# Turning the residual unscaled and by column halves, and scaling the gate and up rows behind the matmul

## The chip, the cores and the metric

One of the eight cores of a Trainium2 chip runs the kernel: TensorE (matmul), VectorE, ScalarE, GpSimd and SyncE, on-chip memory SBUF, and PSUM, eight banks of 128 x 512 floats that TensorE writes. The metric is the device time of one execution in microseconds.

## The reference

Two transformer blocks over 256 tokens of width 1024, all in float32. The first block (three mixers, a mixture of experts and an embedding gate) is not touched. The second has two layers, and each ends in the feed-forward stage that the change is about:

```python
def rmsnorm(x, g):
    var = jnp.mean(xf * xf, axis=-1, keepdims=True)
    return (xf * lax.rsqrt(var + RMS_EPS)).astype(x.dtype) * g

def conv_ffn(h, w_up, w_conv, w_down):
    gu = causal_dwconv(h @ w_up, w_conv)      # 3 taps along the tokens
    g, u = jnp.split(gu, 2, axis=-1)          # D_FF = 2816 columns each
    return (jax.nn.silu(g) * u) @ w_down

for i in range(2):
    h = rmsnorm(x, mix_norm[i])
    x = x + (short_conv_mixer(h, ...) if i == 0 else moba_attention(h, ...))
    x = x + conv_ffn(rmsnorm(x, ffn_norm[i]), ffn_w_up[i], ffn_w_conv[i], ffn_w_down[i])
return rmsnorm(x, final_norm)
```

## The kernel before

Weights come as a stream of 216 units of 128 x 2048 floats. SyncE loads them into four buffers (`raw`). Each matmul is done as three passes of a narrower float format, so each unit is split: ScalarE writes the rounded part `whi`, VectorE the difference `wlo` (`split`, L505 and L1099), into rings of three. A ring slot is free again when TensorE has counted up `unit_used`; a `raw` buffer is loaded again when VectorE has counted up `low_done`. Every engine runs its own list of instructions strictly in order and waits on counters; `split_to(n)` issues all splits up to unit n at that place of the list. The order of all lists is written by hand.

**The turn.** `xres` holds the residual, tokens on partitions, as two tiles of 128 tokens; `add` (L1136) adds a PSUM bank to one half of the columns (512) of one tile. For the next product the residual has to stand with its columns on partitions. So ScalarE squares each half tile and sums it (`norm_act`, L531), GpSimd makes the inverse root `rstd` (`norm_pool`, L1005), VectorE writes `xn = xres * rstd` (`normed`, L1120), TensorE transposes the sixteen 128 x 128 blocks (`turn`, L1869), and ScalarE and VectorE take them out of PSUM with the norm's gain as a high and a low part (`turn_act` L540, `turn_dve` L1126), eight blocks each. Turn 5 stands ahead of feed-forward stage 0 and turn 7 ahead of stage 1.

**The product ahead of a turn.** `dense` (L1896; in the attention layer `o_part`, L2496) makes two chunks of 512 columns, each of two units. Of the second chunk's second unit all products of tile 0 come first (`tile_done`), then those of tile 1 (`unit_used`), so `add_chunks` (L1146) can add the tiles apart.

**A feed-forward stage** (`experts`, L2399) has eleven groups. `group` (L2346) makes 256 gate and 256 up rows from two units: 96 matmuls into two PSUM banks, bank pair by the group's parity. ScalarE then starts the three-tap convolution out of PSUM (L789) and VectorE adds two taps (L1642), 4 + 8 instructions. Then ScalarE's silu, VectorE's product, ScalarE's rounding and VectorE's low part, and `h_ready` lets `down` (L2367) multiply the hidden block by one unit. TensorE's order is group 0, group 1, down 0, group 2, down 1, and so on; `expert_step` (L2391) makes one group and the down product of the group before. ScalarE and VectorE have the unit splits between: `ahead(3)` before a group's convolution, `ahead(4)` behind it, `ahead(5)` behind silu and product. In the first step `ahead(4)` is the second unit of group 1. The last group (`halves_apart`, `ffn_last_act` L802, `ffn_last_dve` L1661) puts the gate and up rows of half 0 in one bank and those of half 1 in the other, and its halves are worked off apart. Ahead of that both engines split unit 32 of the stage, which needs the slot of the last group's first unit.

## Time and profile before

| | |
|---|---|
| median of 3 runs | 1138.96 us (1138.21 to 1139.0) |
| profiled execution | 1140.76 us, its span 1138.9 us |
| TensorE busy | 94% of the span |
| VectorE, ScalarE, GpSimd busy | 74%, 63%, 7% |
| chain that ended last | TensorE 78%, VectorE 13%, ScalarE 4% |
| mean granted TensorE clock | 0.980 of full |

The profiled execution has instruction starts and lengths for every engine. Times count from the span's start. Engines are PE (TensorE), PEld (its weight loads), DVE (VectorE), ACT (ScalarE), POOL (GpSimd), SP (SyncE). A row of the timeline may merge like instructions (x8), and ends, where the engine stood idle before it, with that time and what ended it. A matmul's recorded length includes its way through the array, so matmuls overlap. Stage 0 lies at about 613 to 800 us, stage 1 at 943 to 1131.

### The profile page before, as it was taken

How to read it: one execution, taken by the hardware profiler on the slowest of the kernel's cores; microseconds unless marked ns; L12 is line 12 of the kernel's file. 1: busy time of each engine (PE TensorE's matmuls, PEld its weight loads, DVE VectorE, ACT ScalarE, POOL GpSimd, SP SyncE). 2: the span in 40 equal slices, each digit the busy share in tenths (PEclk: the TensorE clock that was granted, in tenths of full speed). 3: DMA queues.
4: the chain of work that ended last, by engine and by line, in shares of the span. 5: the costliest groups of instructions: out<-in, count | busy, mean ns of one | idle time of the engine just before them, and what ended most of it. 6: DMA issues, size and time to landing. Idle time of an engine off the chain costs nothing.

```text
span 1138.9 us, 17179 instructions
## 1 busy us (share of the span) xinstructions
PE 1076.1 (94%) x6358; PEld 932.5 (82%) x6358; DVE 842.6 (74%) x1084; ACT 713.6 (63%) x947; POOL 76.3 (7%) x82
## 2 busy tenths in 40 slices
PE   7998979999999999889999999999899989999997
PEld 6877867777877787769988899998788868999996
DVE  5498678999899998767654776676867866766765
ACT  6667478888888887665433654454557765554553
POOL 1001100000000000030000110120000011101100
PEclk9999989999999999999999999999999998999999
DMA  9440528888889898645443545554343324555531
GB/s 369 163 161 25 212 82 306 332 333 316 343 320 343 312 352 305 243 157 185 170 168 143 186 173 197 188 185 179 148 148 111 111 96 151 203 198 189 185 142 38
DMA packets 33604, 232.62 MB, mean 204 GB/s; under 512 B 3856, under 2 KB 3984, under 8 KB 6032
## 3 DMA queue, kind: packets, MB, share of 16 engines
q1 hardware_dynamic: 32688, 229.98, 54.6%
q10 hardware_dynamic: 864, 1.93, 0.5%
q8 instruction: 34, 0.56, 0.2%
q14 instruction: 18, 0.15, 0.0%
HBM read 230.85 MB, written 1.05 MB: 204 GB/s over the span
## 4 chain that ended last, share of the span: by engine, by line
PE 78%; DVE 13%; ACT 4%; issue 3%; DMA 2%; POOL 1%; DVEq 0%; ACTq 0%; SPq 0%; POOLq 0%
PE bank L1862 11%; PE bank L1863 11%; PE bank L1864 11%; PE bank L2361 9%; PE bank L2362 9%; PE bank L2363 9%; DVE wlo L1104 5%; PE bank L2218 4%; PE bank L2219 4%; PE bank L2201 2%; DMA raw<-stream 1%; PE bank L2226 1%; PE bank L2267 1%; PE bank L2266 1%; DVE arena L1502 1%
## 5 line engine op out<-in xcount | busy, mean ns | idle before, releaser
L1104 DVE TENSOR_TENSOR wlo<-raw,whi 128x2048 fp32r<-128x2048 f32 x212 | 481.8, 2286 | 85.9 <-ACT whi L514 84.8
L514 ACT ACTIVATE whi<-raw 128x2048 fp32r<-128x2048 f32 x213 | 406.6, 1917 | 122.2 <-PE bank L2363 64.1
L2361 PE MATMUL bank<-xs,whi 128*128 128x256 f32 x896 | 252.2, 282 | 4.5 <-DVE wlo L1104 3.3
L2362 PE MATMUL bank<-xs,whi 128*128 128x256 f32 x896 | 251.3, 280 | 0.0
L2363 PE MATMUL bank<-xs,wlo 128*128 128x256 f32 x896 | 250.8, 280 | 0.0
L2361 PEld LDWEIGHTS bank<-xs,whi 128*128 128x128 f32 x896 | 169.5, 189 | 6.7 <-DVE wlo L1104 3.7
L2362 PEld LDWEIGHTS bank<-xs,whi 128*128 128x128 f32 x896 | 169.6, 189 | 0.8
L2363 PEld LDWEIGHTS bank<-xs,wlo 128*128 128x128 f32 x896 | 169.5, 189 | 0.0
L1862 PE MATMUL bank<-whi,rounded 128*128 128x512 f32 x344 | 139.3, 405 | 5.4 <-DVE rounded L1511 4.9
L1863 PE MATMUL bank<-wlo,rounded 128*128 128x512 f32 x344 | 137.7, 400 | 0.0
L1864 PE MATMUL bank<-whi,rounded 128*128 128x512 f32 x344 | 137.5, 400 | 0.0
L1862 PE MATMUL bank<-whi,xs 128*128 128x512 f32 (+1 forms) x304 | 122.9, 404 | 6.2 <-DVE xs L1625 2.1
L1864 PE MATMUL bank<-whi,xs 128*128 128x512 f32 (+1 forms) x304 | 120.2, 395 | 0.0
L1863 PE MATMUL bank<-wlo,xs 128*128 128x512 f32 (+1 forms) x304 | 120.0, 395 | 0.0
L1646 DVE SCALAR_TENSOR_TENSOR arena<-bank,cwn,arena 128x255 f32<-128x255 f32 (+1 forms) x160 | 66.1, 476 | 68.0 <-ACT arena L790 67.3
L1862 PEld LDWEIGHTS bank<-whi,rounded 128*128 128x128 f32 x344 | 65.7, 191 | 24.5 <-issue 7.5
L790 ACT ACTIVATE arena<-bank,cwn 128x256 f32<-128x256 f32 x80 | 31.4, 476 | 84.8 <-PE bank L2363 84.8
L1864 PEld LDWEIGHTS bank<-whi,rounded 128*128 128x128 f32 x344 | 65.6, 191 | 15.9
L1863 PEld LDWEIGHTS bank<-wlo,rounded 128*128 128x128 f32 x344 | 65.4, 190 | 13.0
L1862 PEld LDWEIGHTS bank<-whi,xs 128*128 128x128 f32 x304 | 58.5, 193 | 19.2 <-issue 3.3
L1864 PEld LDWEIGHTS bank<-whi,xs 128*128 128x128 f32 x304 | 58.2, 192 | 13.4
L1863 PEld LDWEIGHTS bank<-wlo,xs 128*128 128x128 f32 x304 | 58.6, 193 | 11.9
(320 smaller groups left out, 1462.5 us busy)
## 6 DMA issues: line engine op xcount, KB each, us to landing
raw<-stream SPq DMA_DIRECT2D x215, 1024.0 KB, 4.8
arena<-finals ACTq DMA_DIRECT2D x3, 512.0 KB, 3.8
xres<-x_in SPq DMA_DIRECT2D x2, 512.0 KB, 5.0
raw<-stream SPq DMA_DIRECT2D x4, 256.0 KB, 6.2
out<-xn SPq DMA_DIRECT2D x4, 256.0 KB, 2.1
par<-params SPq DMA_DIRECT2D x1, 844.0 KB, 12.5
cst<-table SPq DMA_DIRECT2D x1, 502.0 KB, 8.9
arena<-p_in ACTq DMA_DIRECT2D x1, 256.0 KB, 6.0
```

Of the source, the lines that this page charges most:

```text
L514: act.activation(whi[:, s, :], raw[:, a, :], ACT.Copy).then_inc(S("high_done"), 1)
L790: ins = act.activation(facc[:, b, f, :], bank[2 * gb + f // 2][:, (f % 2) * T:(f % 2 + 1) * T], ACT.Copy, scale=cwn[:, b, 8 + f:9 + f])
L1104: dve.tensor_tensor(wlo[:, s, :], raw[:, unit0 % RAW, :], whi[:, s, :].bitcast(F32), ALU.subtract)\
L1646: ins = dve.scalar_tensor_tensor(a, src[:, 0:T - 2 + k], cwn[:, b, 4 * k + f:4 * k + f + 1], a, ALU.mult, ALU.add)
L1862: pe.matmul(o, ah, bh, start=start, stop=False, skip_group_check=True)
L1863: pe.matmul(o, ah, bl, start=False, stop=False, skip_group_check=True)
L1864: return pe.matmul(o, al, bh, start=False, stop=stop, skip_group_check=True)
L2218: pe.matmul(bank[e][:], tokens, whi[:, s, c], start=kk == 0, stop=False, skip_group_check=True)
L2219: ins = pe.matmul(bank[e][:], tokens, wlo[:, s, c], start=False, stop=kk == 7, skip_group_check=True)
L2361: pe.matmul(o, whi[:, s, w], xhi[:, kk, :], start=first, stop=False, skip_group_check=True)
L2362: pe.matmul(o, whi[:, s, w], xlo[:, kk, :], start=False, stop=False, skip_group_check=True)
L2363: ins = pe.matmul(o, wlo[:, s, w], xhi[:, kk, :], start=False, stop=kk == 7, skip_group_check=True)
```

## The change

- Turns 5 and 7 transpose `xres` itself, not `xn`. They go by column halves: the eight transposes of half 0 stand inside the product ahead (between the units of its second chunk, or between its two tiles), tile 0's other four behind it, tile 1's other four inside group 0, ahead of its block k = 2. `normed` falls away for them.
- The inverse root is put in later. After group 0 TensorE spreads `rstd` along a row of 256 tokens by two matmuls against the identity, and ScalarE copies it out (`root_row`). For every group VectorE multiplies both PSUM banks by this row into `fraw` (two instructions, `rooted`), and all taps read `fraw` in SBUF. TensorE waits for `rooted` instead of `g_free` before it writes the banks again.
- The last group runs in two passes over its two units: first all rows of half 0 (`half_done`), then those of half 1. Its units are let go in the second pass only.
- The splits, adds and turns on ScalarE and VectorE are put in a new order around both turns (below), and two units more are split before the turn or inside it.
- The projection of layer 0 swaps its banks (first chunk 0 and 1, second 2 and 3). Some counters get other names, and the adds of the first block are written out in the order that they had.

```diff
-CHUNK_BANK = {C_PLEG: 0, C_PLEG + 1: 4, C_QKV: 4, C_QKV + 1: 6}
+CHUNK_BANK = {C_PLEG: 0, C_PLEG + 1: 4, C_SCOUT: 0, C_SCOUT + 1: 2, C_QKV: 4, C_QKV + 1: 6}
...
+        fraw = arena[:, 2048:4096].rearrange("p (b f t) -> p b f t", b=2, f=4)
+        root_row = arena[:, 4096:4096 + T]
@@ ScalarE, ffn_act @@
-                act.wait_ge(S("unit_used"), group_end(u0, e, e0))
+                act.wait_ge(S("rooted"), d0 + 1 + e)
...
-                    ins = act.activation(facc[:, b, f, :], bank[2 * gb + f // 2][:, (f % 2) * T:(f % 2 + 1) * T],
-                                         ACT.Copy, scale=cwn[:, b, 8 + f:9 + f])
+                    ins = act.activation(facc[:, b, f, :], fraw[:, b, f, :], ACT.Copy, scale=cwn[:, b, 8 + f:9 + f])
@@ ScalarE, ahead of stage 0 @@
-            split_to(U_SCOUT + 4)
+            split_to(U_FFN0)
+            turn_act(5, range(0, 4))
             norm_act(5, slice(0, 2))
-            split_to(U_SCOUT + 5)
-            norm_act(5, slice(2, 4))
+            split_to(U_FFN0 + 1)
...
+                split_to(u0 + 2)
+                act.wait_ge(S("root_made"), layer + 1)
+                act.activation(root_row, bank[4][:, 0:T], ACT.Copy).then_inc(S("root_ready"), 1)
                 ffn_act(layer, 0, None, 0)
...
-            turn_act(5)
+            turn_act(5, range(4, KD))
+            norm_act(5, slice(2, 4))
             ffn(0)
@@ ScalarE, ahead of stage 1 @@
+            split_to(U_FFN1)
             o_high(7)
-            split_to(U_WO + 4)
-            norm_act(7)
-            split_to(U_WO + 5)
+            split_to(U_FFN1 + 1)
+            turn_act(7, range(0, 4))
+            norm_act(7, slice(0, 2))
+            turn_act(7, range(4, KD))
+            norm_act(7, slice(2, 4))
             act.dma_start(final_g, finals[1]).then_inc(S("final_loaded"), 16)
-            turn_act(7)
             ffn(1)
@@ VectorE, ahead of stage 0 @@
-            add_chunks(U_SCOUT, C_SCOUT, 5, late=True)
+            split_to(U_SCOUT + 3)
+            add_first(C_SCOUT, CHUNK_END[C_SCOUT])
+            split_to(U_FFN0)
+            turn_dve(5, range(0, 4))
+            add_second(C_SCOUT, 5, 0)
+            split_to(U_FFN0 + 1)
+            add_second(C_SCOUT, 5, 1)
+            turn_dve(5, range(4, KD))
@@ VectorE, ffn_dve @@
                 ahead(3)
+                dve.wait_ge(S("unit_used"), group_end(u0, e, e0))
+                if e0 == 0:
+                    dve.wait_ge(S("root_ready"), layer + 1)
+                for half in range(2):
+                    ins = dve.tensor_tensor(fraw[:, b, 2 * half:2 * half + 2, :],
+                                            bank[2 * gb + half][:].rearrange("p (f t) -> p f t", f=2),
+                                            root_row.unsqueeze(1).broadcast_to([P, 2, T]), ALU.mult)
+                ins.then_inc(S("rooted"), 1)
+                dve.wait_ge(S("rooted"), d0 + 1 + e)
                 dve.wait_ge(S("ffn_begun"), layer * FH + 1 + e)
@@ VectorE, ffn_last_dve @@
                 split_to(u0 + 3 * FE - 1)
                 for half in range(2):
+                    dve.wait_ge(*((S("unit_used"), group_end(u0, e, e)) if half else (S("half_done"), layer + 1)))
+                    dve.tensor_tensor(fraw[:, b, half::2, :], bank[2 * gb + half][:].rearrange("p (f t) -> p f t", f=2),
+                                      root_row.unsqueeze(1).broadcast_to([P, 2, T]), ALU.mult)\
+                       .then_inc(S("rooted"), 1)
+                    dve.wait_ge(S("rooted"), d0 + 1 + e + half)
                     dve.wait_ge(S("ffn_begun"), layer * FH + 1 + e + half)
@@ VectorE, ahead of stage 1 @@
+            split_to(U_FFN1)
             o_low(7)
-            add_chunks(U_WO, C_WO, 7, U_WO + 3, late=2)
-            turn_dve(7)
+            add_first(C_WO, U_WO + 3)
+            add_second(C_WO, 7, 0)
+            turn_dve(7, range(0, 4))
+            add_second(C_WO, 7, 1)
             split_to(U_FFN1 + 1)
+            turn_dve(7, range(4, KD))
@@ TensorE @@
+            def turn_tile(q, t, ks):
+
+                for k in ks:
+                    if k % 4 == 0:
+                        pe.wait_ge(S(f"residual{t}_ready"), 2 * q - 1 + k // 4)
+                    ins = pe.transpose(turned_k(q, k)[:, P * t:P * t + P], xres[:, t, P * k:P * k + P], ident)
+                    if t == 1 and k % 2:
+                        ins.then_inc(S("turned"), 1)
@@ group @@
-                for i in range(2):
+                for part_, i in [(p, i) for p in range(2 if halves_apart else 1) for i in range(2)]:
                     s = wait_unit((unit0 + i, off))
                     for k in range(4):
                         kk = 4 * i + k
+                        if kk in ahead_of:
+                            ahead_of[kk]()
                         wait_turned(q, kk)
-                        for at in range(4):
+                        for at in range(2 * part_, 2 * part_ + 2) if halves_apart else range(4):
...
-                    ins.then_inc(S("unit_used"), 1)
+                    if part_ or not halves_apart:
+                        ins.then_inc(S("unit_used"), 1)
+                    elif i:
+                        ins.then_inc(S("half_done"), 1)
@@ expert_step @@
-                pe.wait_ge(S("g_free"), g0 + e)
+                if e0:
+                    pe.wait_ge(S("rooted"), d0 + e)
@@ experts @@
-                group(g0, u0, q)
+                turn_tile(q, 0, range(4, KD))
+                group(g0, u0, q, ahead_of={2: lambda: turn_tile(q, 1, range(4, KD))})
+
+                pe.wait_ge(S("xt_ready"), KD * q + 2)
+                for t in range(TT):
+                    pe.wait_ge(S(f"rstd{t}_ready"), q + 1)
+                    ins = pe.matmul(bank[4][:, P * t:P * t + P], rstd[:, t:t + 1].broadcast_to([P, P]), ident,
+                                    start=True, stop=True, skip_group_check=True)
+                ins.then_inc(S("root_made"), 1)
...
-            for c in range(2):
-                dense(C_SCOUT + c, U_SCOUT + 2 * c, "sc_ready" if c == 0 else None, c == 1)
-            turn(5)
+            dense(C_SCOUT, U_SCOUT, "sc_ready")
+            dense(C_SCOUT + 1, U_SCOUT + 2, None, True, lambda: [turn_tile(5, t, range(4)) for t in range(TT)])
...
             o_part(1, 1, (2, 3), (0,))
+            for t in range(TT):
+                turn_tile(7, t, range(4))
             o_part(1, 1, (2, 3), (1,))
-            turn(7)
```

## Rows read from the trace of the kernel before

**Rows 1.** The page, busy time of each engine over the span.
```profile
PE 1076.1 (94%) x6358; PEld 932.5 (82%) x6358; DVE 842.6 (74%) x1084; ACT 713.6 (63%) x947; POOL 76.3 (7%) x82
```

**Rows 2.** The waits of PE: line, waited-for line, us in total, times, longest.
```profile
PE bank L1884 <- DVE xn L1123: 8.4, 5, 3.9
...
PE bank L2361 <- DVE wlo L1104: 3.3, 2, 1.6
```

**Rows 3.** Timeline of PE at turn 5: start, length, instruction, idle before.
```profile
609.66 1.09 PE L1884 MATMUL bank<-cst,xn 128*128 128x128 f32 x8 [1.18 <-DVE xn L1123]
611.61 1.65 PE L1884 MATMUL bank<-cst,xn 128*128 128x128 f32 x8 [0.85 <-DVE xn L1123]
613.59 0.55 PE L2361 MATMUL bank<-xs,whi 128*128 128x256 f32 x1 [0.32 <-DVE xs L1132]
```

**Rows 4.** Timeline of ACT and DVE around turn 5.
```profile
602.98 1.92 ACT L514 ACTIVATE whi<-raw 128x2048 fp32r<-128x2048 f32 x1 [2.46 <-PE bank L1864]
605.72 0.69 DVE L1138 TENSOR_TENSOR xres<-bank,xres 128x512 f32<-128x512 f32 x1 [4.10 <-PE bank L1864]
...
612.08 3.03 ACT L545 ACTIVATE xs<-bank,par 128x256 fp32r<-128x256 f32 x8 [2.11 <-PE bank L1884]
```

**Rows 5.** Timeline of DVE, PE and ACT at turn 7 and the end of group 0 behind it.
```profile
932.42 2.09 DVE L1138 TENSOR_TENSOR xres<-bank,xres 128x512 f32<-128x512 f32 x3 [2.59 <-PE bank L1864]
...
939.11 3.59 PE L1884 MATMUL bank<-cst,xn 128*128 128x128 f32 x16 [3.92 <-DVE xn L1123]
...
956.04 1.57 ACT L790 ACTIVATE arena<-bank,cwn 128x256 f32<-128x256 f32 x4 [9.75 <-PE bank L2363]
```

**Rows 6.** Timeline of ACT, DVE and PE behind group 0 of stage 0.
```profile
625.89 1.57 ACT L790 ACTIVATE arena<-bank,cwn 128x256 f32<-128x256 f32 x4 [8.97 <-PE bank L2363]
...
627.50 3.34 DVE L1646 SCALAR_TENSOR_TENSOR arena<-bank,cwn,arena 128x255 f32<-128x255 f32 x8 [6.92 <-ACT arena L790]
630.76 2.28 DVE L1104 TENSOR_TENSOR wlo<-raw,whi 128x2048 fp32r<-128x2048 f32 x1
...
633.09 0.38 PE L2361 MATMUL bank<-xs,whi 128*128 128x256 f32 x1 [1.64 <-DVE wlo L1104]
```

**Rows 7.** A PE wait; windows: busy PE, PEld, DVE, ACT, POOL, granted clock, DMA share, GB/s.
```profile
584.30 0.47 PE L1862 MATMUL bank<-whi,xs 128*128 128x512 f32 x1 [2.07 <-DVE xs L1625]
...
585.00:586.00 1.00, 1.00 (x4) 0.81 (x3) 0.95 (x2) 1.00 (x1) 0.00 (x0) 0.50 0.12 49
633.00:634.00 1.00, 0.91 (x7) 0.91 (x8) 1.00 (x3) 0.63 (x2) 0.09 (x1) 1.00 0.00 0
```

**Rows 8.** Timeline of DVE, ACT and PE around the last group of stage 1.
```profile
1108.41 2.28 DVE L1104 TENSOR_TENSOR wlo<-raw,whi 128x2048 fp32r<-128x2048 f32 x1
...
1114.82 1.92 ACT L514 ACTIVATE whi<-raw 128x2048 fp32r<-128x2048 f32 x1 [2.77 <-PE bank L2363]
...
1116.77 2.29 DVE L1104 TENSOR_TENSOR wlo<-raw,whi 128x2048 fp32r<-128x2048 f32 x1 [2.67 <-ACT whi L514]
1121.23 3.47 DVE L1673 SCALAR_TENSOR_TENSOR arena<-bank,cwn,arena 128x255 f32<-128x255 f32 x8 [2.17 <-ACT arena L813]
...
1120.35 1.57 ACT L813 ACTIVATE arena<-bank,cwn 128x256 f32<-128x256 f32 x4 [3.62 <-PE bank L2363]
...
1126.16 0.47 PE L1862 MATMUL bank<-whi,rounded 128*128 128x512 f32 x1 [0.25 <-DVE rounded L1685]
```

**Rows 9.** The page and the groups of lines (count, busy us, mean ns), then one timeline row.
```profile
L1646 DVE SCALAR_TENSOR_TENSOR arena<-bank,cwn,arena 128x255 f32<-128x255 f32 (+1 forms) x160 | 66.1, 476 | 68.0 <-ACT arena L790 67.3
L790 ACT ACTIVATE arena<-bank,cwn 128x256 f32<-128x256 f32 x80 | 31.4, 476 | 84.8 <-PE bank L2363 84.8
...
L867 ACT ACTIVATE arena<-arena,par 128x256 f32<-128x256 f32 x8 | 3.6, 503 | 3.3 <-DVE arena L1606 3.3
L1614 DVE SCALAR_TENSOR_TENSOR arena<-arena,par 128x256 f32<-128x256 f32 x16 | 7.0, 482 | 4.3 <-ACT arena L867 4.2
...
82.88 0.39 PE L2021 MATMUL bank<-arena,cst 128*128 128x128 f32 x2
```

More of the change, by code:

```diff
@@ L538, in norm_act, with turn_act @@
                                    accum_out=sumsq[:, t, c:c + 1]).then_inc(S(f"sumsq{t}_ready"), 1)
-            def turn_act(q):
-                for k in range(KD):
+            def turn_act(q, ks=range(KD)):
+                for k in ks:
                     if k % 2 == 0:
@@ L1124, in normed, with turn_dve @@
                        .then_inc(S(f"xn{t}_ready"), 1)
-            def turn_dve(q):
-                for k in range(KD):
+            def turn_dve(q, ks=range(KD)):
+                for k in ks:
                     if k % 2 == 0:
@@ L1396, in _ @@
             turn_y_dve(2)
-            add_chunks(U_WOUT, C_WOUT, 1, U_WOUT + 3, late=True)
+            split_to(U_WOUT + 4)
+            add_first(C_WOUT, U_WOUT + 3)
+            dve.wait_ge(S("final_loaded"), 16)
+            for t in range(TT):
+                tokens_scaled(t, 0)
+            for t in range(TT):
+                add_second(C_WOUT, 1, t)
+                tokens_scaled(t, 1)
             turn_dve(2)
@@ L1922, in dense @@
                     ins.then_inc(S("unit_used"), 1)
+                    if u == 0 and between:
+                        between()
             pe.wait_ge(S("ident_loaded"), 16)
@@ L2555, in _ @@
             o_part(1, 1, (2, 3), (0,))
+            for t in range(TT):
+                turn_tile(7, t, range(4))
             o_part(1, 1, (2, 3), (1,))
-            turn(7)
             experts(G_FFN1, FH, U_FFN1, FE, 7)
```

86 lines of the change are left out of this document (34 added, 52 removed).

## The prediction

> **What bounds the kernel now.** I read the page's busy shares first. TensorE is busy for 1076 of 1139 us, VectorE for 74% [rows 1]. So relieving VectorE or ScalarE alone can't pay. What can pay is time in which TensorE stands still. The waits of TensorE, read next, show where that is. It waits for `xn` at the transposes five times, 8.4 us in total, and for `wlo` inside the group products twice, 3.3 us [rows 2]. The timeline of the stretches that the diff touches gives the rest.
>
> **Before feed-forward stage 0** the last product of the projection ends at 608.48 (609.66 less 1.18 idle). The first eight transposes start at 609.66, the other eight at 611.61, and the first gate/up product at 613.59 [rows 3]. The two tiles of the projection's second column half end one after the other. Its first half ends at about 602.7, tile 0 at 605.7, and the adds follow [rows 4]. The rest of the pause is squares on ScalarE, the inverse root on GpSimd, and the scaling by it on VectorE. **Before stage 1** it is the same pause, longer: products end at 935.19 (939.11 less 3.92), sixteen transposes run from 939.11 to 942.70, and the group ends at 956.04 [rows 5].
>
> **Inside a stage** the steady step is bound by TensorE: two units of a group and one of a down product, 5.6 us each (the two units of the last group are let go at 1114.82 and 1120.35, the down products end at 1125.91) [rows 6, 8]. A step is 16.8 us. The exceptions are the first step and the last. In the first, the second unit of group 1 can't be split before the taps of group 0, since VectorE has that split behind them: group 0 is handed over at 625.89, the split starts at 630.76, and TensorE goes on at 633.09 after 1.64 us idle [rows 6]. In the last, TensorE waits only 0.25 us for the hidden block [rows 8].
>
> **The change, part by part.** All sums are against the profiled execution, 1140.76 us with a span of 1138.9; the median of the runs shown, 1138.96, lies 1.8 below it, and I carry the difference over to it.
>
> *1. The turn by halves.* Eight transposes take 1.09, the last of them 0.27 long, so one each 0.117 us and eight 0.94 [rows 3]. Eight now stand in the middle of the projection's second half, where their input (column half 0) has been added long before. Four stand behind it and four inside group 0, ahead of its third block of rows. I followed each input. In stage 0 tile 0's second half is ready at 607.4 and needed at 609.4. Tile 1's is late, because VectorE has the split of the group's second unit before that add, and ScalarE's half of that split stands behind four turned blocks (from 603.7, 0.38 each [rows 4]) and two squares (twice as wide, 0.65 each by my estimate). It runs at about 606.5 to 608.4, so VectorE splits until 610.7 and adds until 611.4. TensorE asks at 612.5, so 1.1 us of cover are left; without it each us late costs a us. In stage 1 VectorE adds at once and the cover is 1.6 us. So group 0 should follow the transposes with no pause and at full clock. A group at full clock is 2 x 5.55 us and 0.2 for its last product to leave, 11.3. Its end comes at 608.48 + 0.94 + 0.94 + 11.3 = 621.7 instead of 625.89, and at 935.19 + 1.88 + 11.3 = 948.4 instead of 956.04 [rows 5, 6]. **Gain 4.2 + 7.7 = 11.9 us.** The clock that is lost now behind these pauses is in it.
>
> *2. Scaling behind the matmul* is not free. For the first group of a stage TensorE spreads the root over the partitions by two fp32 products. One with 128 columns is recorded as two parts, 0.22 together [rows 9], so 0.44. ScalarE copies the row out (0.48, as its other 256-wide evictions [rows 9]). VectorE multiplies two banks; three 128x512 adds out of PSUM take 2.09 [rows 5], so two about 1.35. Only then come ScalarE's four taps and VectorE's eight. All of it is on the chain that sets the split of group 1's second unit: 0.44 + 0.48 + 1.35 + 0.15 for three hand-overs, 2.4 us more. The unit starts 9.6 us after the group instead of 7.2, and TensorE, which has 5.85 us of work, stands for 3.75 us instead of 1.64. The ends of the 2.4 are 1.9, with the spreading products at one pass each like a transpose and the multiplications at 0.48, and 2.8, with 0.1 us lost at each hand-over. I take 2.4, since each term is nearest to its row. **Cost 2.4 x 2 = 4.8 us.** The root itself is squared and raised while group 0 runs (ScalarE and GpSimd have little else there), so it isn't late.
>
> In the steady steps VectorE had three splits, taps and two products, 3 x 2.28 + 3.34 + 2 x 0.69 = 11.6 us of 16.8 [rows 6]; now 12.9. The second unit's split is done 8.8 us after the group and needed at 11.2, the hidden block at 12.3 and needed at 16.8. No cost; the cover is 2.4 us.
>
> The eight taps now read SBUF. The nearest rows are the short convolution's: 482 ns for a tap from SBUF against 476 from PSUM, and on ScalarE 503 against 476 [rows 9]. I take no gain and 0.1 us of loss within the hand-overs. The Trainium skill (VectorE: DVE Perf Modes, "The TRN2 errata") gives VectorE 62 cycles at 0.96 GHz less for an SBUF source than for a PSUM one, and ScalarE 52 cycles at 1.2 GHz more. By that estimate the four tap chains would be 0.35 us shorter each, and the sum 1.4 us lower. The rows agree for ScalarE in direction (+27 ns) and not for VectorE.
>
> *3. The last group in two passes.* Its first pass (gate and up rows of half 0) ends after 5.6 us, which looks like an early start. But both passes need both units. The second unit is wanted 2.8 us into the group instead of 5.6. Its split ended at 1110.69 [rows 8] and is now 1.4 us later, 1112.15, against a need at 1111.75: 0.4 us of stall. And the first unit is let go only at three quarters of the group: 1118.0 instead of 1114.82. Both ScalarE and VectorE have the split of the last down unit (unit 32 of the stage) ahead of everything of the last group. ScalarE's part then ends at 1119.95, VectorE's at 1122.25 (1119.05 now, before the group had ended). Only there can VectorE multiply half 0 by the root. From there the two engines take turns, since the second half's multiplication is queued behind the first half's taps: 0.69 + 0.85 + 1.74, and again, + five hand-overs of 0.05, is 6.8; the product, rounding and low part take 1.4 more, as they do now (taps end at 1124.7, TensorE goes on at 1126.16) [rows 8]. Of this chain no row shows the multiplication by a row; it is priced by the add out of PSUM, 0.69, and by a plain 256-wide tap at the lower end, 0.48. That is 1130.4. TensorE has work until 1126.15, so it stands for 4.2 us. **Cost 4.2 x 2 = 8.4 us** (the 0.4 is in it).
>
> *4. The clock.* After 2.07 us idle the granted clock stands at 0.50 of full, 1.2 GHz; after 1.64 us it stays at 1.00, 2.4 GHz [rows 7]. So the two pauses that the change removes give it back (counted in 1), while four new ones, of 3.75 and 4.2 us, should each lose it. A pause that does costs, by the rows, 1.5 us in stage 0 (eight transposes 1.65 instead of 1.09, the group 12.3 instead of 11.3) and 3.4 in stage 1 (3.59 instead of 1.87, 13.1 instead of 11.3) [rows 3, 5, 6]. Behind dense products the lower one is nearer, since the slow stretch begins while TensorE still waits. **Cost 4 x 1.5 = 6.0 us**, ends 0 and 4 x 3.4.
>
> *5. What is moved.* VectorE's scaling of `xn` falls away (four of 0.45 per stage), off the path after the change. ScalarE and VectorE split the stage-1 unit ahead of the last head's block; both stand idle there, waiting for the last head's products, which covers it; without that the split would delay the block by its 1.9 us. The transfer of the final gains is issued behind all squares instead of ahead of the turn; it is wanted 180 us later. The weight loads on SP's queue are released by VectorE's splits, which lie up to 6 us earlier ahead of a stage and later at its end by the pauses; four buffers cover that. The banks of the projection are swapped so that group 0's are free first. The renamed semaphores and the first block's rewritten adds keep their order: nothing.
>
> **Sum.** -11.9 + 4.8 + 8.4 + 6.0 = **+7.3 us**: 1148.1 for a profiled execution, **1146.3** for the median.
>
> **The rivals.** *A, the forecast*: chance 0.64. With 1.0 to 1.8 us of clock per pause (the loss within the two groups that follow a pause now) and the ends of the first-step chain, its own range is 1143.3 to 1148.7.
> *B, the pauses come but the clock mostly stays*: +1.3, 1140.3. For it: a pause of 1.64 us didn't cost it. Against: pauses of 2.07 and 3.92 us did. 0.12.
> *C, faster*: VectorE reaches half 0 of the last group when the first pass ends, and the tail is hidden. Then that cost and its clock are gone, -11.9 + 4.8 + 3.0 - 0.5 = -4.6, 1134.4. It turns on one point, whether the last down unit's split is behind VectorE by then; by my times it ends 7 us too late. For it: ScalarE and VectorE idle 3 us ahead of the split [rows 8]. 0.08.
> *D, part of the front gain is lost* to tile 1's late add, or a steady step loses its 2.4 us of cover: 2 to 4 us more, 1149 to 1151. 0.10.
> *E, the turn doesn't hide at all* (the change doesn't do what it says): the pauses stay, +17 or more. 0.06.
>
> A difference of 0.2% (2.3 us) is about what a measurement of this kernel tells from none. Faster: C, 0.08. Within: nearly all of B, 0.12. Slower: A, D, E, 0.80. The range holds A, B and D and leaves out C and E: 1140 to 1151.
>
> **What would show it.** Step 1: no idle row before the transposes, group 0 of the stages ending near 621.7, and 7.7 us early again in stage 1, clock 1.00 there. Step 2: `root_row` and `fraw` rows ahead of the taps, and TensorE waiting about 3.7 us for `wlo` in each stage's group 1. Step 3: in each last group the `wlo` split runs into the down product, and TensorE waits about 4 us for the hidden block. Step 4: four new stretches at 0.50. It is wrong if the tail wait is under 1 us, if the clock stays at 1.00 behind such waits, or if the first wait doesn't grow.

## The result

The changed kernel takes **1150.76 us** (median of 4 runs, 1150.33 to 1152.41) against 1138.59 of the kernel before (4 runs on the same chip). The ratio is 1.0107 [1.0081, 1.0133]: slower, by 12.2 us, where +7.3 was forecast and 1140 to 1151 was the range. Its profiled execution took 1150.95 us, with a span of 1148.8.

The page and the waits of PE in the changed kernel:

```profile
PE 1079.9 (94%) x6366; PEld 936.5 (82%) x6366; DVE 868.9 (76%) x1120; ACT 715.9 (62%) x949; POOL 138.7 (12%) x82
```
```profile
PE bank L1883 <- DVE rounded L1704: 8.7, 2, 4.3
PE bank L2395 <- DVE wlo L1112: 8.2, 4, 3.7
```

Against [rows 2]: the waits for `xn` at turns 5 and 7 are gone, the waits for `wlo` went from 3.3 to 8.2 us, and the one for the low part of the hidden block (`rounded`) ahead of the last down product grew from 0.2 us in each stage to 4.3. The timeline of PE, changed kernel, at the landmark (the wait of [rows 7], ahead of both turns), turn 5, the root, the two first-step waits, the last group, its tail, and turn 6:

```profile
581.79 0.47 PE L1883 MATMUL bank<-whi,xs 128*128 128x512 f32 x1 [2.07 <-DVE xs L1625]
...
600.21 1.04 PE L1895 MATMUL bank<-cst,xres 128*128 128x128 f32 x8
...
606.67 0.60 PE L1895 MATMUL bank<-cst,xres 128*128 128x128 f32 x4
...
609.92 0.60 PE L1895 MATMUL bank<-cst,xres 128*128 128x128 f32 x4
...
618.76 0.61 PE L2445 MATMUL bank<-cst,rstd 128*128 128x128 f32 x4
...
628.66 0.58 PE L2395 MATMUL bank<-xs,whi 128*128 128x256 f32 x1 [3.68 <-DVE wlo L1112]
...
636.81 0.40 PE L1883 MATMUL bank<-whi,rounded 128*128 128x512 f32 x1
...
798.80 0.77 PE L1883 MATMUL bank<-whi,rounded 128*128 128x512 f32 x1 [4.35 <-DVE rounded L1704]
...
809.09 0.44 PE L1914 MATMUL bank<-cst,xn 128*128 128x128 f32 x2 [1.79 <-DVE xn L1132]
...
963.17 0.58 PE L2395 MATMUL bank<-xs,whi 128*128 128x256 f32 x1 [3.67 <-DVE wlo L1112]
...
971.30 0.39 PE L1883 MATMUL bank<-whi,rounded 128*128 128x512 f32 x1
...
1114.65 0.38 PE L2395 MATMUL bank<-xs,whi 128*128 128x256 f32 x1 [0.40 <-DVE wlo L1112]
...
1133.33 0.77 PE L1883 MATMUL bank<-whi,rounded 128*128 128x512 f32 x1 [4.34 <-DVE rounded L1704]
```

Four rows of the kernel before, same engine, that answer to them (down 0, the start of the last down product and turn 6 of stage 0, down 0 of stage 1):

```profile
638.80 0.39 PE L1862 MATMUL bank<-whi,rounded 128*128 128x512 f32 x1
...
796.00 0.47 PE L1862 MATMUL bank<-whi,rounded 128*128 128x512 f32 x1 [0.24 <-DVE rounded L1685]
...
803.77 0.45 PE L1884 MATMUL bank<-cst,xn 128*128 128x128 f32 x2 [1.93 <-DVE xn L1123]
...
968.95 0.39 PE L1862 MATMUL bank<-whi,rounded 128*128 128x512 f32 x1
```

The pauses ahead of the turn are gone: the transposes at 600.21, 606.67 and 609.92 have no idle time before them. Cut at these rows, the two executions compare as follows. (The changed kernel's execution reached the first landmark 2.5 us earlier, 581.79 against 584.30, in code that is the same in both; that lead is not the change's, and in the eleven other kernels below the same landmark lies between 580.83 and 587.44.)

| stretch | before | after | difference | forecast |
|---|---|---|---|---|
| landmark to group 1 resumed | 48.79 | 46.87 | -1.9 | -4.2 + 2.4 = -1.8 |
| to down 0 | 5.71 | 8.15 | +2.4 | clock, 1.5 |
| to the start of the last down product | 157.20 | 161.99 | +4.8 | 4.2 |
| to turn 6 | 7.77 | 10.29 | +2.5 | clock, 1.5 |
| to down 0 of stage 1 | 165.18 | 162.21 | -3.0 | -7.7 + 2.4 + 1.5 = -3.8 |
| to the start of the last down product | 157.21 | 162.03 | +4.8 | 4.2 |
| to the span's end | 12.7 | 15.5 | +2.8 | clock, 1.5 |
| sum | 554.6 | 567.0 | +12.4 | +7.3 |

Two terms are off. The stretches behind a pause, where TensorE does the same work as before, are 2.4 to 2.8 us longer instead of 1.5. And a last group costs 4.8 instead of 4.2. The windows around the pauses of stage 0, changed kernel (busy time of each engine, granted clock, DMA share, GB/s):

```profile
622.00:625.00 3.00, 2.98 (x26) 2.77 (x24) 1.93 (x5) 2.98 (x5) 0.00 (x0) 1.00 0.00 0
...
628.70:630.00 1.30, 1.30 (x6) 1.30 (x7) 1.30 (x2) 0.93 (x3) 1.30 (x1) 0.50 0.21 32
...
630.00:633.00 3.00, 3.00 (x16) 3.00 (x16) 3.00 (x3) 1.68 (x1) 3.00 (x1) 0.50 0.95 350
635.00:638.00 3.00, 3.00 (x23) 2.78 (x23) 0.99 (x2) 0.00 (x0) 0.00 (x0) 1.00 0.95 363
794.00:797.00 3.00, 0.45 (x2) 0.01 (x1) 1.92 (x5) 1.21 (x3) 0.00 (x0) 1.00 0.23 96
...
800.00:803.00 3.00, 3.00 (x8) 2.32 (x8) 2.29 (x1) 2.37 (x2) 0.00 (x0) 0.50 0.00 0
806.00:809.00 3.00, 1.30 (x6) 0.73 (x4) 2.47 (x5) 2.78 (x8) 0.99 (x3) 1.00 0.37 156
```

16 matmuls in the 3 us behind the pause, 23 and more at full clock.

The chain of the first step, ACT and DVE in stage 0, changed kernel:

```profile
619.41 0.38 ACT L884 ACTIVATE arena<-bank 128x256 f32<-128x256 f32 x1 [4.48 <-PE bank L2445]
...
621.22 1.71 ACT L793 ACTIVATE arena<-arena,cwn 128x256 f32<-128x256 f32 x4 [1.43 <-DVE arena L1652]
```
```profile
619.90 1.29 DVE L1652 TENSOR_TENSOR arena<-bank,arena 128x512 f32<-128x512 f32 x2 [2.64 <-ACT arena L884]
623.03 3.37 DVE L1661 SCALAR_TENSOR_TENSOR arena<-arena,cwn 128x255 f32<-128x255 f32 x8 [1.85 <-ACT arena L793]
626.32 2.29 DVE L1112 TENSOR_TENSOR wlo<-raw,whi 128x2048 fp32r<-128x2048 f32 x1
```

This is step 2 as forecast: root row, multiplication, taps, and only at 626.32 the split for which TensorE waits until 628.66. The tail of stage 1, same engines:

```profile
1120.67 1.92 ACT L517 ACTIVATE whi<-raw 128x2048 fp32r<-128x2048 f32 x1 [4.71 <-PE bank L2397]
1125.63 0.91 ACT L815 ACTIVATE arena<-arena,cwn 128x256 f32<-128x256 f32 x2 [3.04 <-DVE arena L1684]
```
```profile
1122.62 2.29 DVE L1112 TENSOR_TENSOR wlo<-raw,whi 128x2048 fp32r<-128x2048 f32 x1 [4.62 <-ACT whi L517]
1124.83 0.68 DVE L1684 TENSOR_TENSOR arena<-bank,arena 128x512 f32<-128x512 f32 x1
1126.64 1.79 DVE L1692 SCALAR_TENSOR_TENSOR arena<-arena,cwn 128x255 f32<-128x255 f32 x4 [1.13 <-ACT arena L815]
1128.35 0.68 DVE L1684 TENSOR_TENSOR arena<-bank,arena 128x512 f32<-128x512 f32 x1
1130.08 1.79 DVE L1692 SCALAR_TENSOR_TENSOR arena<-arena,cwn 128x255 f32<-128x255 f32 x4 [1.04 <-ACT arena L815]
...
1132.77 0.99 DVE L1704 TENSOR_TENSOR rounded<-arena,rounded 128x256 fp32r<-128x256 f32 x2
```

Half 0 of the gate and up rows stands finished in its bank, and VectorE stands idle 4.62 us ahead of the split of the last down unit, which ScalarE can only begin when the second pass lets the unit's slot go. Everything of the last group is queued behind it.

### The profile page after: what moved, and what is told of

It reads as the page before. It is cut to its first block, busy times and chain, and to the rows that moved or that the text cites. A ratio compares the mean times of both kernels' runs of the same rounds, so it can differ in the third digit from the quotient of the medians.

```text
span 1148.8 us, 17257 instructions
## 1 busy us (share of the span) xinstructions
PE 1079.9 (94%) x6366; PEld 936.5 (82%) x6366; DVE 868.9 (76%) x1120; ACT 715.9 (62%) x949; POOL 138.7 (12%) x82
## 3 DMA queue, kind: packets, MB, share of 16 engines
q10 hardware_dynamic: 864, 1.93, 0.6%
## 4 chain that ended last, share of the span: by engine, by line
PE 78%; DVE 13%; ACT 5%; issue 3%; POOL 1%; DMA 0%; DVEq 0%; ACTq 0%; POOLq 0%
PE bank L1883 11%; PE bank L1884 10%; PE bank L1885 10%; PE bank L2395 9%; PE bank L2396 9%; PE bank L2397 9%; DVE wlo L1112 5%; PE bank L2250 5%; PE bank L2251 4%; PE bank L2233 2%; ACT whi L517 1%; PE bank L2299 1%; PE bank L2298 1%; PE bank L2258 1%; DVE arena L1502 1%
## 5 line engine op out<-in xcount | busy, mean ns | idle before, releaser
L1883 PE MATMUL bank<-whi,rounded 128*128 128x512 f32 x344 | 141.9, 413 | 13.7 <-DVE rounded L1704 8.7
L1885 PE MATMUL bank<-whi,rounded 128*128 128x512 f32 x344 | 138.9, 404 | 0.0
L1078 POOL COPY cwn<-par 128x12 f32 (+1 forms) x22 | 103.8, 4725 | 200.4 <-DVE arena L1661 200.2
L1661 DVE SCALAR_TENSOR_TENSOR arena<-arena,cwn 128x255 f32<-128x255 f32 (+1 forms) x160 | 66.7, 479 | 38.7 <-ACT arena L793 38.0
L793 ACT ACTIVATE arena<-arena,cwn 128x256 f32<-128x256 f32 x80 | 34.2, 498 | 96.8 <-DVE arena L1652 96.8
L1883 PEld LDWEIGHTS bank<-whi,rounded 128*128 128x128 f32 x344 | 66.7, 194 | 33.2 <-issue 15.5
L1016 POOL TENSOR_SCALAR total<-sumsq 128x1 f32<-128x1 f32 x14 | 7.2, 515 | 692.3 <-ACT xn L539 691.9
L1883 PEld LDWEIGHTS bank<-whi,xs 128*128 128x128 f32 x304 | 58.2, 191 | 20.2 <-issue 3.0
## 6 DMA issues: line engine op xcount, KB each, us to landing
par<-params SPq DMA_DIRECT2D x1, 844.0 KB, 12.4
```

Of the source, the lines that this page charges most:

```text
L1078: pool.tensor_copy(cwn[:, b, :], src).then_inc(S("taps_ready"), 1)
L1661: ins = dve.scalar_tensor_tensor(a, fraw[:, b, f, 0:T - 2 + k], cwn[:, b, 4 * k + f:4 * k + f + 1], a, ALU.mult, ALU.add)
L1883: pe.matmul(o, ah, bh, start=start, stop=False, skip_group_check=True)
L1885: return pe.matmul(o, al, bh, start=False, stop=stop, skip_group_check=True)
```

## The experiments

Eleven kernels, each timed in turn with the kernel before, whose median was 1137.7 to 1138.6 us in these comparisons. TensorE's waits at the four places, read from the timeline of each (stage 0; stage 1 agrees within 0.03 us where it has the place), and the medians:

| kernel | first step | last group | its tail | turn 6 | median us | ratio to before |
|---|---|---|---|---|---|---|
| before | 1.64 | 0 | 0.24 | 1.93 | 1138.59 | |
| changed | 3.68 | 0.40 | 4.35 | 1.79 | 1150.76 | 1.0107 [1.0081, 1.0133] |
| e1 one pass | 3.67 | 0 | 2.95 | 1.78 | 1144.75 | 1.0066 [1.0052, 1.0081] |
| e2 half 0 first | 3.67 | 0.40 | 0 | 3.62 | 1141.16 | 1.0033 [1.0021, 1.0044] |
| e3 early split | 1.27 | 0.40 | 4.33 | 1.79 | 1141.77 | 1.0034 [1.0021, 1.0047] |
| e4 both | 1.27 | 0.40 | 0 | 3.62 | 1130.87 | 0.9946 [0.9930, 0.9962] |
| e5 before + early split | 0 | 0 | 0.24 | 1.93 | 1134.21 | 0.9967 [0.9951, 0.9983] |
| e6 whole turn | 3.68 | 0.40 | 4.33 | 1.80 | 1152.79 | 1.0129 [1.0108, 1.0151] |
| e7 filled pauses | filled | 0.40 | filled | 1.94 | 1143.53 | 1.0040 [1.0024, 1.0056] |
| e8 root twice | 3.67 | 1.59 | 4.33 | 1.78 | 1151.61 | 1.0111 [1.0091, 1.0131] |
| e9 four places | 2.22 | 0.40 | 0 | 2.16 | 1134.03 | 0.9962 [0.9950, 0.9975] |
| e10 root early | 3.21 | 0.40 | 4.36 | 1.79 | 1148.48 | 1.0086 [1.0066, 1.0106] |
| e11 third split | 0.53 | 0.40 | 0 | 2.17 | 1128.31 | 0.9912 [0.9891, 0.9933] |

My theory going in: the gain of the turn is there in full, and the whole loss is four pauses, made by two splits that stand in the wrong place of a queue, and the slow clock behind them, which I had priced too low. Rivals: the passes or the two-engine chain itself bind the tail; VectorE's longer chain slows the steady steps; the slow stretches aren't the clock's.

### The tail: e1 and e2

```diff
-                for part_, i in [(p, i) for p in range(2 if halves_apart else 1) for i in range(2)]:
+                for i in range(2):
```

> The changed kernel with the last group of each stage in one pass over its two units, as before the change: a unit is let go when it has been used, VectorE's two row multiplications both follow the end of the group. Everything else as in the changed kernel. The prediction's step 3 says that the two passes let the first unit go 3 us later and so put the last down unit's split, and with it the whole tail, later. By it the split ends 3 us earlier but half 0 can't be scaled before the group's end, about 1120.4 on the scale of before: the tail stall shrinks from 4.35 to about 2.7 and the 0.4 us stall for the second unit goes. TensorE keeps the half clock behind a stall of 2.7 us. Expected: 1.6 to 2 us less for each stage, 3 to 4 less in all, 1147 against 1150.8. Rival: the passes help, since half 0 is ready earlier; then the stall is as long or longer and the time 1151 to 1154.

1144.75 us, 6 less than the changed kernel, where 3 to 4 were expected. The tail wait is 2.95 and the one of 0.40 gone, as expected. From down 0 to down 9, the one behind the last group, stage 0 takes 151.2 us with one pass, as before the change, and 151.9 with two: the passes cost 0.7 us a stage in themselves, and 1.4 more by what they make late. That is 4.2 of the 7.2 us between the profiled spans. The rest is clock: the stretch behind the tail is 1.1 us shorter than in the changed kernel in each stage, and in stage 0 the one behind the first step's pause, which this edit doesn't touch, 0.9.

```diff
# e2, both engines, last group (VectorE's list shown)
-                split_to(u0 + 3 * FE - 1)
                 for half in range(2):
...
+                    if half:
+                        split_to(u0 + 3 * FE - 1)
                     dve.wait_ge(S("ffn_begun"), layer * FH + 1 + e + half)
...
-                for half in range(2):
                     dve.wait_ge(*((S("g_free"), g0 + 1 + e) if half else (S("half_tapped"), layer + 1)))
...
```

Silu, product, rounding and low part of a half now stand behind its own taps, in one loop with them.

> The changed kernel, but in the last group of each stage ScalarE and VectorE take half 0 (row multiplication, taps, SiLU, product, rounding, low part) ahead of the last down unit's split, which then stands on both engines between half 0 and half 1. The first pass ends 5.6 us into the group, so half 0 needs no wait for the split. If the queued split is what made the tail late (my explanation of step 3), TensorE's wait for the hidden block goes from 4.35 us to under 0.5, and with it the slow clock behind it (2.7 to 3 us): 7 us less for each stage, 1150.8 - 14 = 1137. Rival: the tail is bound by the chain of half 1 after the group's end, not by the split; then the stall stays near 4 us for the second half and the time falls by 0 to 3.

The tail wait is 0 in both stages, so the queued split was what made it. The gain is 9.6 us, not 14. Where the rest went shows at turn 6, in the timeline of e2:

```profile
798.38 2.29 DVE L1112 TENSOR_TENSOR wlo<-raw,whi 128x2048 fp32r<-128x2048 f32 x1 [1.38 <-ACT whi L517]
800.58 1.88 DVE L1147 TENSOR_TENSOR xres<-bank,xres 128x512 f32<-128x512 f32 x3
```
```profile
804.33 0.55 PE L1913 MATMUL bank<-cst,xn 128*128 128x128 f32 x3 [3.62 <-DVE xn L1132]
```

With the tail's pause gone, the residual's adds are held up by the split of the next unit in VectorE's list, and TensorE waits 3.62 us instead of 1.79 and loses the clock there (0.50 from 806 to 812). In the changed kernel the adds came behind the last down product, which had started late and ran slowly, and that covered the split.

### The first step: e3, e4, e5

```diff
             def ffn(layer):                     # VectorE; ScalarE: split_to(u0 + 2) -> split_to(u0 + 3)
+                split_to(u0 + 3)
                 ffn_dve(layer, 0, None, 0)
```

> The changed kernel, but the split of group 1's second unit stands ahead of the scaling of group 0 on ScalarE and VectorE, where both have time while group 0 runs. If step 2 is right, the stall of 3.7 us in the first step is that split being queued behind group 0's whole chain, and it goes; group 0's chain itself is then wanted only by the down product, 11.2 us after the group. Expected: 3.7 us of stall and 3 us of clock less for each stage, 1150.8 - 13.4 = 1137.4. Rival: the unit's load isn't there yet or the buffer isn't free, so that both engines stand at the split and group 0's chain is late: stall for the hidden block instead, gain under 4 us.

9.0 us less, of 13.4 expected. The wait for `wlo` is gone; the one that is left, 1.27, is for the hidden block, whose chain my expectation had ready in time. The clock stays at 1.00 behind it.

> Both edits in one kernel: group 1's second split ahead of group 0's scaling, and half 0 of the last group ahead of the last down unit's split. If the four pauses and the clock behind them are the whole price of the change, what is left is its gain alone: 1150.8 - 13.4 - 14 = 1123.5, which is 1.3% under the kernel before; the granted clock stays at 1.00 through both stages. Rival: other costs are in the 12 us (steady steps slower by the longer VectorE chain, transfers); then it stays above 1130.

1130.87 us: **0.5% under the kernel before**, and 7.4 over the expectation, just above the 1130 of its rival. The trace accounts for most of the 7.4 without the rival's costs. New waits are 4.3, 1.27 twice and 1.8 more at turn 6. Clock lost at turn 6 is 1.2: from turn 6 to down 0 of stage 1, without the wait there, e4 takes 157.3 us and e3, whose clock stays at 1.00, 156.0. And the expectation had put some 3 us of clock on each of the four pauses, 12 in all, where the table above shows 10.2.

> The kernel before with one edit alone, the split of group 1's second unit ahead of group 0's taps on ScalarE and VectorE. It had 1.64 us of stall there in each stage without loss of clock. Expected: 1.64 x 2 = 3.3 us under the kernel before, 1135.3. Rival: nothing, since the split, put ahead, delays the hidden block or meets a weight load that isn't there: 1138 to 1140.

1134.21, 4.4 less than before. It takes away both waits of 1.64 us (3.3); the other 1.1 lies within the interval, which goes from 1.9 to 5.6 us less. So over two fifths of what the best version below gains over the kernel before has nothing to do with the change; the old kernel could have had it.

### What the turn's gain consists of: e6

The adds of both tiles, then all sixteen transposes of `xres`, then group 0; scaling behind the matmul as in the changed kernel.

> The changed kernel with the unscaled residual, but turned whole: all sixteen transposes stand between the projection's last product and group 0, behind both tiles' adds, as they stood before the change but without the wait for the root. It parts the gain of step 1 into what comes from leaving the root out and what from the halves. By the rows the transposes then wait for the last add only, about 1 us after the last product, and eight transposes more (0.94 us) lie in the open: 1.5 to 2.5 us more for each stage than in the changed kernel, 1154 to 1156, and no slow clock before the group. Rival: most of the gain is from the halves: 4 to 7 us more for each stage, 1159 or above, with the clock lost before the group.

In stage 0 the sixteen transposes follow the projection without idle time, since those of tile 0 cover the add of tile 1. TensorE waits behind them, 0.88 us, for the first turned blocks. From the landmark to the resumed group 1 it takes 47.97 us (582.39 to 630.36) against 46.87 with halves, and 48.79 + 2.04 = 50.83 if the old turn had had the longer first-step wait too. So of the 4.0 us gained in stage 0, 2.9 come from not waiting for the root (with the clock that this wait cost) and 1.1 from the halves. The median is 2.0 us above the changed kernel, 1.0 for each stage where 1.5 to 2.5 were expected.

### The clock: e7

15 matmuls of 512 columns (the expectation says 256; their number and time are right) ahead of group 1's second unit and 18 ahead of the last down product, into banks that aren't in use; their result isn't read.

> The changed kernel with products whose result isn't used in the four pauses: 15 of 256 columns ahead of group 1's second unit, 18 ahead of the last down product. They are extra work; the result is unchanged. They last about as long as the pauses (15 x 0.23 = 3.5 us, 18 x 0.23 = 4.2 us) and TensorE never stands for 2 us. If the clock is lost by the standing still, it stays at 1.00 behind all four and the 11.2 us that I read as loss of clock come back while the pauses stay: 1150.8 - 11 = 1139.6. Rival: the slower stretch behind a pause is something else (weight loads, memory): the time stays at 1150 or rises by what the fill oversteps, and the records behind the pauses stay long.

The fill and the windows behind the filled pauses, e7:

```profile
L2433 PE MATMUL bank<-xs 128*128 128x512 f32 x15 | 3.6, 392 | 0.0
```
```profile
634.00:637.00 3.00, 3.00 (x28) 3.00 (x27) 3.00 (x3) 2.33 (x2) 3.00 (x1) 1.00 0.80 262
...
801.00:804.00 3.00, 2.91 (x13) 2.40 (x14) 1.52 (x2) 3.00 (x3) 0.00 (x0) 1.00 0.01 3
...
810.00:812.00 2.00, 1.87 (x9) 1.53 (x8) 0.81 (x2) 0.80 (x3) 0.00 (x0) 0.50 0.00 0
```

The pauses are as long as before, and behind them the clock stays at 1.00. Landmark to down 0 takes 52.6 us (586.44 to 639.06) instead of 55.0, down 0 to turn 6 169.8 instead of 172.3, down 0 of stage 1 to the end 2.7 less: 2.4, 2.5 and 2.7 back, which is what the table above shows as lost there. The fourth, 2.4, is hidden behind a new loss: turn 6's own pause, 1.94 us, now costs the clock (0.50 at 810 to 812), which the changed kernel's 1.79 us there did not. So the slow stretches are the clock's, and they go when TensorE doesn't stand still. The median fell by 7.2, not 11. The profiled execution, 1147.49, is the slowest of ten; five of them took 1140.2 to 1142.8 at a mean granted clock of 0.981 to 0.986, the profiled one had 0.977. By these the expectation of 1139.6 is nearly met where the clock holds; that it is the pause at turn 6 which parts the two groups isn't shown, since only one was profiled.

### The cover of the steady steps: e8

```diff
                 ins.then_inc(S("rooted"), 1)    # e0 >= 2: ahead of it, both multiplications once more
```

> The changed kernel with the multiplication by the root row done twice in every steady step of the loop, the second result into room that nobody reads: 1.3 us more on VectorE in each of 8 steps of a stage. By step 2's sum VectorE has 2.4 us of cover there, so nothing changes: 1150 to 1152. Rival: VectorE already bounds the steady step, and the change lost time there: 1.3 us x 16 = up to 20 us more.

1151.61, 0.9 above the changed kernel, within what can be told from none. In the steady steps TensorE never waits, so at least 1.3 of the 2.4 us of cover are there. One place does feel it, the last group, in the timeline of e8:

```profile
784.59 0.38 PE L2400 MATMUL bank<-xs,whi 128*128 128x256 f32 x1 [1.59 <-DVE wlo L1112]
```

0.40 grew by 1.19 for 1.3 us of work: there the two passes have used the cover up, which my expectation overlooked. The same run shows that a pause's price isn't fixed. TensorE goes on at 632.75, after 3.67 us as in the changed kernel, but the clock falls only afterwards (windows of e8):

```profile
632.80:634.00 1.20, 1.20 (x10) 1.20 (x11) 1.20 (x2) 0.83 (x3) 1.20 (x1) 1.00 0.19 27
635.00:637.00 2.00, 2.00 (x11) 2.00 (x11) 2.00 (x3) 0.76 (x1) 2.00 (x1) 0.50 0.96 401
638.00:640.00 2.00, 2.00 (x19) 2.00 (x19) 0.30 (x1) 0.00 (x0) 0.36 (x1) 1.00 1.00 397
```

From there to down 0 it takes 7.27 us (640.02) instead of the changed kernel's 8.15 and 5.71 without loss. So the same pause costs 1.6 us of clock in one execution and 2.4 in another, and a slightly shorter one none at all (e10, next).

### The root row's hand-over: e10

The two spreading products stand ahead of block k = 7 of group 0.

> The changed kernel with the two products that spread the root moved from behind group 0 to ahead of its last block of rows; the root is there by then. It tests the first two terms of step 2's chain (0.44 for the products, 0.48 for the copy, and two hand-overs). The products still cost TensorE 0.44, only earlier. VectorE should multiply right at the group's end, 0.9 us sooner, and group 1 be resumed 0.45 us sooner after 3.2 us of stall instead of 3.68, in each stage: 1150.8 - 0.9 = 1149.9, more or less 1.5 for the clock. Rival: the chain is bound by ScalarE or the tap weights, and the first-step stall stays at 3.68 or grows by the 0.44.

3.21 us of stall, 0.47 less; 1148.48. The chain of step 2 is the one that binds, and its first two terms have the size that they were given. The stalls explain 0.9 of the 2.3 us by which the median fell; the rest is clock at least in part. In stage 0 TensorE goes on at 632.97 and is at down 0 at 638.68, 5.71 us later, so the pause of 3.21 us cost no clock; in stage 1, behind 3.20, it takes 7.27. And behind turn 6's pause of 1.79 us, which cost nothing in the changed kernel, the clock is lost (windows of e10, behind the first step's pause and behind turn 6's):

```profile
633.00:636.00 3.00, 3.00 (x26) 3.00 (x26) 3.00 (x3) 2.62 (x3) 3.00 (x1) 1.00 0.61 197
...
812.00:815.00 3.00, 2.74 (x10) 2.27 (x11) 1.78 (x5) 2.36 (x7) 0.00 (x0) 0.50 0.00 0
```

### Clearing what e4 left: e9 and e11

```diff
# e9 and e11, ScalarE, last group
                     ins.then_inc(S("ffn_begun"), 1)
+                    if half:
+                        split_to(u0 + 3 * FE)
# e9, both engines, first step: ahead(5) behind the rounding and behind the low part
# e11 instead, ScalarE: split_to(u0 + 4) ahead of root_row; VectorE:
                 dve.wait_ge(S("rooted"), d0 + 1 + e)
+                if off is None and e0 == 0:
+                    split_to(u0 + 4)
```

> The kernel with both reorderings, and two more places cleared that its trace shows. In the first step the rounding and the low part of the hidden block stand ahead of the next split on both engines: TensorE waited 1.27 us for that block behind the split, in each stage. At the end of a stage ScalarE's half of the first unit behind the stage stands in its 3.3 us of idle time, so that VectorE's half ends 1.3 us earlier and the residual's adds, which it held up, begin earlier: the pause before the next turn goes from 3.62 to about 2.3 us. Expected: 2 x 1.27 + 1.3 = 3.8 us less by stalls, and 0 to 2 us of clock, 1130.9 - 4.5 = 1126.4. Rival: the pauses only move on to the next split behind, and the time stays within 1.5 us of 1130.9.

1134.03, 3.2 above e4, a miss. Turn 6's pause shrank as meant, 3.62 to 2.16. But in the first step the wait grew from 1.27 to 2.22: `ahead(5)` there is the split of the down unit itself, and TensorE needs both it and the hidden block. Putting one ahead only makes the other the last:

```profile
629.39 4.49 DVE L1117 TENSOR_TENSOR wlo<-raw,whi 128x2048 fp32r<-128x2048 f32 x2 [1.11 <-ACT whi L517]
```

It begins 1.11 us after VectorE was free, since ScalarE's half had moved behind the rounding too; TensorE goes on at 631.83, and the clock falls behind it. In stage 1 the wait is 2.23 us and the clock stays at 1.00.

> The kernel with both reorderings and the cleared end of stage 0, but in the first step the down unit's split itself goes ahead instead of behind the hidden block: ScalarE's half stands ahead of the root row's copy, where it is idle for 2.7 us, and VectorE's between the root multiplication and the taps, where it is idle for 1.85 us. The run before it showed that TensorE waits there for whichever of the two, hidden block or down unit, comes last. Now the hidden block should be ready at about 11.0 us after the group and the unit long before, against a need at 11.8: no stall in the first step, 1.27 us less than with both reorderings alone in each stage, and 1.3 to 1.5 at the end of stage 0: 1130.9 - 2.5 - 1.4 = 1127.0, give or take 2 for the clock. Rival: the third split makes the taps late and the hidden block with them; then the stall stays at 1 us or more and the time at 1130 to 1134.

**1128.31 us, 0.9% under the kernel before** and 22 under the changed one. The timelines of DVE and PE in e11: the split stands where VectorE waited for ScalarE's taps, and the wait for the hidden block is 0.53.

```profile
623.15 2.29 DVE L1114 TENSOR_TENSOR wlo<-raw,whi 128x2048 fp32r<-128x2048 f32 x1
```
```profile
631.63 0.50 PE L1887 MATMUL bank<-whi,rounded 128*128 128x512 f32 x1 [0.53 <-DVE rounded L1677]
...
643.65 0.38 PE L2399 MATMUL bank<-xs,whi 128*128 128x256 f32 x1 [0.55 <-DVE wlo L1114]
```

0.55 us are new at group 2's second unit, a step on: the third split didn't vanish, it used the cover of the next step. Against e5, the old kernel with the one edit that it could have had too, the change in this order is worth 5.7 to 5.9 us (-4.4 and -10.1, each against the kernel before on its own chip; 1134.21 to 1128.31). What e11's other moves would give the old kernel wasn't run; its trace in e5 has no wait left in the first step and 0.24 us at the tail, so they have little to take there except at turn 6.

## Why the prediction was right, and where its sizes were off

The pauses came where they were forecast, by the chains that were forecast. The number is a closer thing. 1150.76 lies 0.2 us inside the range, one of the four runs (1152.41) lies above it, and the forecast's own range, A's, ended at 1148.7. The band that holds the result is D's, and D's mechanism didn't happen. That the range held is in good part luck.

- **Step 1, the turn.** Right. No idle time before the transposes in either stage; with the first-step chain the landmark stretch changed by -1.9 for -1.8, and the one to stage 1 by -5.4 without its clock (-3.0 - 2.4) for -5.3. Rival E is out. D's late add didn't happen: tile 1's four transposes follow at 609.92 without idle time. e6 adds what the forecast left open, that leaving out the root is most of it. Some of the gain is clock that the kernel before happened to lose: e5 turns as it does, with the same waits (1.18, 0.84 and 3.92), and takes 1.1 us less from the landmark to down 0 and 1.9 less from turn 6 to down 0 of stage 1, its missing first-step waits counted out.
- **Step 2, the first step.** Right: 3.68 and 3.67 us of stall for 3.75, by the chain as named; e3 takes the split out of it, e10 shortens its head. The multiplication took 1.29 for both banks (1.35), the copy 0.38 (0.48). Taps from SBUF cost VectorE 3.37 us for eight against 3.34 in [rows 6]: no gain, as taken. The Trainium skill's lower figure for an SBUF source (VectorE: DVE Perf Modes, "The TRN2 errata") isn't what this trace shows.
- **Steady steps.** Right as far as tried; e8 puts 1.3 us more in each without a wait.
- **Step 3, the last group.** The place, the cause and the stall were right: 0.40 for 0.4, 4.35 for 4.2. The term was 4.2 and measured 4.8: I had put the 0.4 into the 4.2, but it comes on top, since the first wait moves the passes and the chain alike, and both passes together last 0.3 longer. e2 shows that the queued split decides, which is the point on which rival C turned; C was right about what would happen if the split weren't there.
- **Step 4, the clock.** The mis-sized term. All four pauses lost it, as forecast, but each cost 2.4 to 2.8 us, not 1.5 (2.4, 2.4, 2.5 with a turn-6 wait that is 0.14 shorter, and 2.8): 10.2 for 6.0, which is four of the five microseconds missed. (2.5 is the table's difference; without the shorter wait it is 2.7.) I had taken the lower of two rows, with the reason that the slow stretch begins while TensorE still waits. The reason doesn't hold its weight: in the changed kernel it does begin in the wait, and is still there over 4 us behind it (window 630 to 633). e7 gives the measure directly. But the price is also this execution's: sixteen pauses of the same length, 3.67 or 3.68 us in the first step and 4.33 to 4.36 at the tail, in e1, e2, e3, e6, e8 and e10, cost 1.4 to 2.6 us each by the same reckoning, 2.0 on average. So 1.5 was too low by about 0.5 a pause, and the other 0.5 is what the profiled execution of the changed kernel paid above that; what decides it isn't shown. (The upper end of the step, 3.4, adds up to 3.5 by its own rows.) Rival B is out.
- **Step 5, moved things.** Nothing of them shows as a wait of TensorE.

The profiled executions differ by 10.2 us and the medians by 12.2; the 2.5 us by which the changed kernel's was ahead at the landmark are about the difference.

## What to carry to other kernels

When a step of a chain is made longer or split in two, look at what is queued behind it on the same engine: here 11 us of gain at the turns (4.0 and 7.4, with 3.0 of it clock that e5 didn't lose) became a net loss of 12 by two splits that stood one place too early or too late. Moving them, with no work saved, gave 20 us back, and 22 with the two further moves of e11. Clear a pause and read the trace again, since its neighbour was hidden by it (turn 6 behind the tail, the down unit behind the hidden block). And price a pause with the clock behind it: here 3.7 to 4.4 us of standing cost 1.4 to 2.8 us more. One execution shows one draw of that price.

## What the runs showed of the hardware that wasn't expected

- **Which pause costs the clock isn't set by its length alone.** Ahead of turn 6 the kernel before stands for 1.93 us (row 803.77 above) and keeps 1.00; e7 stands for 1.94 at the same place and gets 0.50. There, too, 1.78 to 1.79 us were followed by 1.00 in the changed kernel, e1 and e3, and 1.78 to 1.80 by 0.50 in e6, e8 and e10. The landmark's 2.07 us, the same in all thirteen executions, were followed by 0.50 in twelve and by 1.00 in e8. 2.22 and 3.20 us lost the clock where 2.23 and 3.21 in the other stage of the same execution didn't (e9, e10). None of 1.27, 1.59, 1.64 and 1.65 was followed by 0.50; 1.18 and 0.85 us with eight transposes between them were, at turn 5 before the change, and not in e5. A difference of 1 to 2 us between two orders of one kernel can be this alone.
- **GpSimd's copies of the tap weights** take 5.5 us in the changed kernel and 2.1 in the one before, the same instruction on the same data. The groups of POOL in the middle of stage 0, before and changed:

```profile
L1070 POOL COPY cwn<-par 128x12 f32 (+1 forms) x8 | 16.6, 2080 | 114.2 <-DVE arena L1646 114.2
```
```profile
L1078 POOL COPY cwn<-par 128x12 f32 x7 | 38.3, 5475 | 77.5 <-DVE arena L1661 77.5
```

The page's POOL went from 76 to 139 us. The change gave the taps two operands from SBUF, where one was PSUM, but that isn't the reason as it stands: a copy starts only when the taps have ended, 0.2 us behind them, and what VectorE does next is the same in both kernels: split, product, split, low part. The copy ends right behind one of these: at 663.15 before the change, 0.06 us behind the first split, and at 666.06 in the changed kernel, 0.05 behind the low part. The Trainium skill (SBUF — State Buffer, "Who interferes with whom") says that a VectorE instruction with two SBUF inputs contends with a GpSimd instruction that reads SBUF. Ends like these agree with it, since all four have two such inputs, but why the copy gets through behind the first of them in one kernel and only behind the fourth in the other isn't shown. Nobody waited for these copies.
